# Stick-breaking attention with two heads interleaved, the weight product on GpSimd and 64-column value products

## The reference, cut to what matters

```python
z = jnp.einsum("bhqd,bhkd->bhqk", q_blk, k_pre) * scale
log_rest = jnp.where(strict, jax.nn.log_sigmoid(-z), 0.0)
suffix = lax.cumsum(log_rest, axis=3, reverse=True) - log_rest
a = jnp.where(strict, jnp.exp(jax.nn.log_sigmoid(z) + suffix), 0.0)
outs.append(jnp.einsum("bhqk,bhkd->bhqd", a, v_pre))
```

## Time and profile before

| | |
|---|---|
| median of 3 runs | 2082.38 us |
| time of the profiled execution | 2080.96 us |
| its span, first to last instruction | 2079.2 us |
| busy in the span | PE 2001.2, DVE 1369.4, ACT 884.9, POOL 499.6 us |
| mean granted TensorE clock | 0.99 |
| attention stage, first scan to end of last scan | 871.7 to 1027.5 us |
| first matmul of the output projection | 1034.35 us |

### The profile page before, as it was taken

One profiled execution on the slowest core, in us unless ns is written; L12 is line 12 of the kernel. 1 busy time (PEld: TensorE's weight loads), 2 busy tenths in 40 slices (PEclk: granted clock), 3 DMA queues, 4 the chain that ended last, 5 costly groups with the idle time before them and its releaser, 6 DMA issues. The chain is left out here.

```text
span 2079.2 us, 25150 instructions
## 1 busy us (share of the span) xinstructions
PE 2001.2 (96%) x9345; PEld 1665.9 (80%) x9345; DVE 1369.4 (66%) x1861; ACT 884.9 (43%) x1571; POOL 499.6 (24%) x360
## 2 busy tenths in 40 slices
PE   6999999999999899898899999999999999999997
PEld 5788888887887688787778888887788888878886
DVE  6765565569798532589745565557755655669896
ACT  6433434434445211477634344443434333334443
POOL 1354555430002121000021100121544554510000
PEclk8999999999999999899999999999999999999999
DMA  4223222254400231343234422231232222265102
GB/s 142 81 71 92 81 76 87 86 195 160 146 21 1 86 102 61 102 91 77 54 94 131 132 82 61 62 111 31 84 89 87 82 78 84 77 238 178 61 1 81
DMA packets 216465, 190.14 MB, mean 91 GB/s; under 512 B 7532, under 2 KB 171928, under 8 KB 216344
## 3 DMA queue, kind: packets, MB, share of 16 engines
q1 hardware_dynamic: 216256, 188.51, 29.4%
q10 hardware_dynamic: 88, 0.02, 0.0%
HBM read 152.85 MB, written 35.65 MB: 91 GB/s over the span
## 5 line engine op out<-in xcount | busy, mean ns | idle before, releaser
L1783 DVE TENSOR_TENSOR w_lo<-st,w_hi 128x512 fp32r<-128x512 f32 x160 | 173.2, 1083 | 178.6 <-ACT w_hi L1362 178.5
L917 PE MATMUL ps<-T_hi,w_lo 128*128 128x512 f32 x640 | 249.3, 390 | 0.3 <-issue 0.3
L918 PE MATMUL ps<-T_lo,w_hi 128*128 128x512 f32 x640 | 249.1, 389 | 0.0
L919 PE MATMUL ps<-T_hi,w_hi 128*128 128x512 f32 x640 | 249.1, 389 | 0.0
L917 PE MATMUL ps<-tr_hi,sr_lo 128*128 128x512 f32 x616 | 242.0, 393 | 5.0 <-DVE xT L2014 2.7
L918 PE MATMUL ps<-tr_lo,sr_hi 128*128 128x512 f32 x616 | 240.0, 390 | 0.0
L919 PE MATMUL ps<-tr_hi,sr_hi 128*128 128x512 f32 x616 | 239.9, 389 | 0.0
L917 PE MATMUL ps<-B_hi,w_lo 128*128 128x512 f32 x576 | 227.0, 394 | 10.8 <-DVE B_lo L1783 4.5
L919 PE MATMUL ps<-B_hi,w_hi 128*128 128x512 f32 x576 | 225.9, 392 | 0.0
L918 PE MATMUL ps<-B_lo,w_hi 128*128 128x512 f32 x576 | 225.7, 392 | 0.0
L871 POOL TENSOR_TENSOR ssq<-sq 128x512 f32<-128x512 f32 x6 | 9.5, 1585 | 612.1 <-issue 425.6
(11 more groups left out here) (252 smaller groups left out, 4359.6 us busy)
## 6 DMA issues: line engine op xcount, KB each, us to landing
gate_raw<-in_ffn_w_gate SPq DMA_DIRECT2D x44, 512.0 KB, 5.4
up_raw<-in_ffn_w_up SPq DMA_DIRECT2D x44, 512.0 KB, 5.2
h_spill<-up_s SPq DMA_DIRECT2D x66, 256.0 KB, 2.0
piece_A<-in_ffn_w_down SPq DMA_DIRECT2D x32, 512.0 KB, 4.6
piece_B<-h_spill SPq DMA_DIRECT2D x32, 512.0 KB, 6.0
wa_raw<-in_w_in SPq DMA_DIRECT2D x16, 512.0 KB, 3.9
wb_raw<-in_w_out SPq DMA_DIRECT2D x16, 512.0 KB, 3.9
wb_raw<-in_mem_w_kv SPq DMA_DIRECT2D x16, 512.0 KB, 3.8
```

Of the source, the lines that this page charges most:

```text
L917: pe.matmul(to, w_lo, m_hi, start=first, stop=False, skip_group_check=joins)
L918: pe.matmul(to, w_hi, m_lo, start=False, stop=False, skip_group_check=joins)
L919: return pe.matmul(to, w_hi, m_hi, start=False, stop=last, skip_group_check=joins)
L1783: return dve.tensor_tensor(to, value, plain(hi), ALU.subtract)
```

## The change

- **Two heads at a time.** Tiles come in fours: blocks 0, 1 of head 2p, then 0, 1 of head 2p + 1, then 6, 7 of both, 2, 3 of both, 4, 5 of both. So 16 tiles make one pass (n = 1, 2, 1, 2, 7, 8, 7, 8, 3, 4, 3, 4, 5, 6, 5, 6), and there are 4 passes. q and k have four places for heads in place of two, and aT has 24 blocks in place of 12.
- **Values in column halves.** values(w) handles two heads and two blocks at once: 2b + 2 steps of two matmuls, each of 64 columns of v, one into PSUM rows 0 to 63 and one into rows 64 to 127. There are 16 such calls in place of 32, with as many matmuls in all (160). The splits act_hi and act_lo take all 128 rows, 16 times each in place of 32.
- **Scan.** Its second data operand (whose operation is bypass) is one PSUM column, broadcast, in a bank that nothing writes meanwhile (STILL_BANK).
- **Product on GpSimd.** beta times rest moves from DVE to POOL (pool.tensor_tensor).
- **Transposes.** The lag goes from 3 to 4 tiles. There are two banks in turn in place of three. For tiles with i >= 4 the first four blocks are now copied by DVE (by_dve), the rest by ACT as before.
- **beta in five places** in place of four. Values start 9 tiles behind the scores, and their splits come 10 behind (OUT_LAG), one step after the values on PE.
- **Loads.** A pair's q and k are loaded two pairs ahead, and the first weights of the output projection once 48 tiles' scores are done. The first two tiles of the output projection wait for the last two value splits in the middle of their sums.

```diff
@@ -598,17 +600,36 @@
             holds.update((b, m) for b in range(*z_bank[m]))
         assert all(end <= 4 for _, end in z_bank)
+        def long_tiles(m):
+
+            return sum(tile_at(k)[1] >= 4 for k in range(m + 1))
+
+        STILL_BANK = a_bank[A_PROJ + 4]
+        TURN_BANKS = [b for b in (4, 5, 6) if b != STILL_BANK]
+        assert STILL_BANK != 7
+
         def turns(m):
-
             i = tile_at(m)[1]
-            return [(turns_before[m] + n, 4 + (turns_before[m] + n) % 3, 4 * n, min(4 * n + 4, i + 1))
+            return [(turns_before[m] + n, TURN_BANKS[(turns_before[m] + n) % 2], 4 * n, min(4 * n + 4, i + 1))
                     for n in range(i // 4 + 1)]
+        turn_of = [(m, first) for m in range(M) for _, _, first, _ in turns(m)]
+
+        def by_dve(m, first):
+
+            return tile_at(m)[1] >= 4 and first == 0
+
+        def turned(nth):
+
+            m, first = turn_of[nth]
+            return (s_aT_dve, long_tiles(m)) if by_dve(m, first) else (s_aT, m + 1)
+
         def aT_part(buf, m, lo_, hi_):
-
-            first = AT_FIRST[tile_at(m)[1] // 2]
+            h, i = tile_at(m)
+            first = AT_FIRST[i // 2] + h % 2 * (i // 2 * 2 + 2)
             return buf[:, first + lo_:first + hi_, (m % 2) * P:(m % 2 + 1) * P]
-        STICK_LAG, TURN_LAG, VALUE_LAG = 1, 3, 6
+
+        STICK_LAG, TURN_LAG, VALUE_LAG, OUT_LAG = 1, 4, 9, 10
         def next_splits(m, p):
...
@@ -904,6 +926,13 @@
                     else:
                         ins.then_inc(s_wsum, 1)
+
+            for m in range(M):
+                n = (tile_at(m)[1] + 1) * P
+                pool.wait_ge(s_sig, 2 * (m + 1))
+                pool.wait_ge(s_scan, m + 1)
+                pool.tensor_tensor(beta[m % BETAS][:, 0:n - 1], beta[m % BETAS][:, 0:n - 1], rest[:, m % 3, 1:n],
+                                   ALU.mult).then_inc(s_a, 1)
             for q in range(4, 8):
                 for c in range(DC):
...
@@ -1192,67 +1221,71 @@
                 h, i = tile_at(m)
-                if m % TC == 0:
-                    pe.wait_ge(s_stack[h % 2], 96 * (h // 2 + 1))
+                slot, g = h // 2 % 2, h % 2
+                if m % (2 * TC) in (0, 2):
+                    pe.wait_ge(s_stack[slot][g], 96 * (h // 4 + 1))
+                queries = q_stack[slot][:, g, i * P:(i + 1) * P]
                 if z_free_after[m]:
                     pe.wait_ge(s_sig, 2 * z_free_after[m])
                 n = (i + 1) * P
                 for lo in range(0, n, HALF):
                     keys = slice(lo, min(n, lo + HALF))
                     z = ps[:, z_bank[m][0] + lo // HALF, 0:keys.stop - lo]
-                    pe.matmul(z, q_stack[:, h % 2, i * P:(i + 1) * P], k_lo2[:, h % 2, keys],
-                              start=True, stop=False)
+                    pe.matmul(z, queries, k_lo2[slot][:, g, keys], start=True, stop=False)
                     if keys.stop == n:
                         pe.matmul(ps[:, z_bank[m][0] + lo // HALF, i * P - lo:n - lo], ident_r, neg,
                                   start=False, stop=False)
-                    mm = pe.matmul(z, q_stack[:, h % 2, i * P:(i + 1) * P], k_hi2[:, h % 2, keys],
-                                   start=False, stop=True)
+                    mm = pe.matmul(z, queries, k_hi2[slot][:, g, keys], start=False, stop=True)
                 mm.then_inc(s_z, 1)
             def turn(m):
                 pe.wait_ge(s_a, m + 1)
                 for nth, bank, first, end in turns(m):
-                    if nth >= 3:
-                        pe.wait_ge(s_aT, nth - 2)
+                    if nth >= 2:
+                        pe.wait_ge(*turned(nth - 2))
                     for j in range(first, end):
                         mm = pe.transpose(ps[:, bank, (j - first) * P:(j - first + 1) * P],
-                                          beta[:, m % 4, j * P:(j + 1) * P], ident[:])
+                                          beta[m % BETAS][:, j * P:(j + 1) * P], ident[:])
                     mm.then_inc(s_aT_ps, 1)
             def values(w):
-                h, b = pair_at(w)
-                pe.wait_ge(s_aT, turns_before[2 * w + 2])
+                hp, b = group_at(w)
+                pe.wait_ge(s_aT, 4 * w + 4)
+                if b >= 2:
+                    pe.wait_ge(s_aT_dve, long_tiles(4 * w + 3))
                 if w:
                     pe.wait_ge(s_o_free, w)
-                pair = slice((h // 2) * P, (h // 2 + 1) * P)
-                o = ps[:, 7, (w % 2) * 2 * P:(w % 2 + 1) * 2 * P]
-                for j in range(2 * b + 2):
-                    lo = P if j == 2 * b + 1 else 0
-                    block = AT_FIRST[b] + j
-                    mm = pe.matmul(o[:, lo:], v_all[:, j, pair], aT[:, block, lo:], start=j == 0, stop=j == 2 * b + 1)
+                n = 2 * b + 2
+                for j in range(n):
+                    lo = P if j == n - 1 else 0
+                    for g in range(2):
+                        o = ps[64 * g:64 * (g + 1), 7, (w % 2) * 2 * P:(w % 2 + 1) * 2 * P]
+                        mm = pe.matmul(o[:, lo:], v_all[:, j, hp * P + 64 * g:hp * P + 64 * (g + 1)],
+                                       aT[:, AT_FIRST[b] + g * n + j, lo:], start=j == 0, stop=j == n - 1)
                 mm.then_inc(s_o, 1)
             pe.wait_ge(a_free, z_banks_free)
             pe.wait_ge(s_neg, 2)
             pe.wait_ge(s_ident_r, 1)
-            for s in range(M + VALUE_LAG):
+            for s in range(M + OUT_LAG):
                 if s < M:
                     scores(s)
-                if s < TURN_LAG:
+                if s < len(pool_among):
                     for k in pool_among[s]:
                         pool_map(k)
                 if s == TURN_LAG:
                     pe.wait_ge(a_free, len(a_units))
                 if 0 <= s - TURN_LAG < M:
                     turn(s - TURN_LAG)
-                if s >= VALUE_LAG and (s - VALUE_LAG) % 2 == 0:
-                    values((s - VALUE_LAG) // 2)
-
-
-            pe.wait_ge(s_aT, turns_before[M])
-            pe.wait_ge(s_o_free, W - 2)
+                if VALUE_LAG <= s < M + VALUE_LAG and (s - VALUE_LAG) % 4 == 0:
+                    values((s - VALUE_LAG) // 4)
+
+
+            pe.wait_ge(s_aT, M)
+            pe.wait_ge(s_aT_dve, long_tiles(M - 1))
+            pe.wait_ge(s_o_free, W - 4)
             for step in B_STEPS:
                 k = b_first[step]
                 if step[0] == "tile":
...
@@ -1654,10 +1687,10 @@
                     act.activation(rest[:, s % 3, 0:n], z, ACT.Sigmoid, scale=-SB_SCALE).then_inc(s_sig, 1)
                     if s < NG:
                         act.wait_ge(s_pl, 2 * (s + 1))
-                    if s >= 4:
-                        act.wait_ge(s_aT_ps, turns_before[s - 3])
-                    act.activation(beta[:, s % 4, 0:n], z, ACT.Sigmoid, scale=SB_SCALE).then_inc(s_sig, 1)
-                if s < TURN_LAG:
+                    if s >= BETAS:
+                        act.wait_ge(s_aT_ps, turns_before[s - BETAS + 1])
+                    act.activation(beta[s % BETAS][:, 0:n], z, ACT.Sigmoid, scale=SB_SCALE).then_inc(s_sig, 1)
+                if s < len(pool_among):
                     for k in pool_among[s]:
                         empty(("unit", k))
                 m = s - TURN_LAG
...
@@ -1666,19 +1699,19 @@
                         act.wait_ge(s_spill[slot], 32 * (2 * SBW // P))
                 if 0 <= m < M:
                     for nth, bank, first, end in turns(m):
+                        if by_dve(m, first):
+                            continue
                         act.wait_ge(s_aT_ps, nth + 1)
-                        if m % 2 == 0 and first == 0 and m >= 4:
-                            act.wait_ge(s_o, m // 2 - 1)
+                        if m >= 8:
+                            act.wait_ge(s_o, m // 4 - 1)
                         copy(aT_part(aT, m, first, end),
-                             ps[:, bank, 0:(end - first) * P].rearrange("p (j t) -> p j t", t=P)
-                             ).then_inc(s_aT, 1)
-                if s >= VALUE_LAG and (s - VALUE_LAG) % 2 == 0:
-                    w = (s - VALUE_LAG) // 2
-                    h, b = pair_at(w)
-                    rows = slice(64 * (h % 2), 64 * (h % 2 + 1))
+                             ps[:, bank, 0:(end - first) * P].rearrange("p (j t) -> p j t", t=P)).then_inc(s_aT, 1)
+                if s >= OUT_LAG and (s - OUT_LAG) % 4 == 0:
+                    w = (s - OUT_LAG) // 4
+                    hp, b = group_at(w)
                     act.wait_ge(s_o, w + 1)
-                    copy(a_hi_t[b // 2][rows, h // 2, b % 2 * 2 * P:(b % 2 + 1) * 2 * P],
-                         ps[rows, 7, (w % 2) * 2 * P:(w % 2 + 1) * 2 * P]).then_inc(s_o_hi, 1)
+                    copy(a_hi_t[b // 2][:, hp, b % 2 * 2 * P:(b % 2 + 1) * 2 * P],
+                         ps[:, 7, (w % 2) * 2 * P:(w % 2 + 1) * 2 * P]).then_inc(s_o_hi, 1)
```

(52 more changed lines are left out.)

31 lines of the change are left out of this document (16 added, 15 removed).

## The result

The changed kernel takes **2085.69 us** (median of 20 runs, 2081.78 to 2087.70) against 2081.61 us (20 runs, 2078.72 to 2085.80) for the kernel before: ratio 1.0017, 95% interval 1.0011 to 1.0023. By the forecast's bound of 0.3% that is no change, on the slow side. The forecast was 2066.4, so it was wrong by 19.3 us. The profiled execution has a span of 2084.9, 5.7 above the one before, where the prediction had 16.0 less: 21.7 us to find.

The account below looks back on a forecast made before the run. DVE was taken to bound the stage: 28.8 us of work, 5.7 of waits, gaps and switches made 35.1 a pass against 39.1. Four passes save 16.0: 2080.96 to 2065.0, plus 1.4 gives 2066.4 us; range 2042 to 2094.

Parts of the forecast that it names:

- rival D: POOL's product or its latency binds, or scans pay for POOL beside them: the 4.0 eaten, 2082 us; chance 0.06.
- the term for the switches: PE switching between full and half width may lose matmul overlap: 0 to 1.9 us a pass, taken as 0.6.
- Rival A: Value halves on PE run one after the other: pass 42.3 us, 2097 in all; chance 0.20.
- "5.7" for the waits: DVE runs dry at three places of a pass, walked through the engines' queues: 5.7 us a pass.
- 1, values of b = 3: In the 5, 6, 5, 6 group DVE waits behind PE's values and ACT's act_hi: 2.7 us a pass.
- 2, values of b = 2, and the scan before it: In the 7, 8, 7, 8 group, 6.0 us on PE and ACT against two scans of 4.3: DVE waits 1.7.
- 3, n = 1, 2 beside long turns: With two banks, short tiles wait for DVE's copy and PE's turn: 0.3, and 1.0 behind b = 1's values.
- gaps, switches, late starts: Added to each pass: 0.5 us of gaps, 0.6 for the switches and 0.3 for late starts.
- rival B: PE's waits drop its clock to half, once a pass: 2.5 us each, 10 later, 2076 us; chance 0.14.
- "The end has one more step, but DVE's product is gone from it: 0, plus or minus 2": At the stage's end the added step and the removed DVE product cancel: 0 us, plus or minus 2.
- C: Queues shift until DVE never runs dry: 29.0 us a pass, 40 us less, 2042 in all; chance 0.12.
- the chance of 0.12 for "no change": Chance that the whole kernel measures within about 0.3% (6.2 us) of before, between 2076.2 and 2088.6 us.

Follow-up runs that it names:

- g6: e4 with every value matmul at the full 128 columns of v, both heads added into the same rows: 2086.69 us.
- e4: e1 with the values 11 and their splits 12 tiles behind, in place of 9 and 10: 2066.79 us.
- i1: e4 with ACT's act_hi a step earlier and DVE's split of the output projection's weights a step later: 2057.89 us.
- g5: e4 with the scan's second operand in SBUF again in place of PSUM: 2093.18 us.
- g7: e4 with the product of beta and rest back on DVE, POOL idle: 2107.12 us.
- e2: e1 with PE's waits for transpose banks filled by three unread float32 matmuls at four points of a pass: 2068.25 us.
- e1: The changed kernel with the output projection's first two weights split in step M + 3 in place of M + 2: 2081.27 us.

## Why the prediction was wrong

**The work was right.** DVE: 28.8 forecast less 0.8 for overlap, 27.1 measured (copy 0.68, split 0.42, scans unchanged). POOL: 23.3 forecast, 19.2 measured, inside the bounds of 17.0 to 24.8, and hidden. One of rival D's signs is there, ACT's rest waiting for POOL's product (0.81 at 943.61 and 1.00 at 963.78 in the second pass), but DVE's scans of these two tiles (945.89 and 966.41) start without a wait. ACT: 25 forecast, 25.5. Halves side by side: right (g6 puts their worth at 5.5 us a pass on e4). A call of halves is 0.15 us longer than one in full width, 3.39 against 3.24, and it begins 0.06 to 0.09 later behind the transposes ahead of it (six transposes take 0.77 to the call in i1 and 0.71 in the kernel before, eight take 0.99 in e4 and 0.90 in g6). Four calls a pass make some 0.9, where the term for the switches was 0.6. The Trainium skill (TensorEngine Tiling (Array Packing), Key Properties) says that a change of the tiling mode drains TensorE; if it did, the drain is within these 0.2 us a call. Rival A is refuted by the row at 974.34. D is refuted by the scans' mean of 1340 ns and by g5 and g7, which are slower.

**The step that failed first is "5.7" for the waits**, in two ways. Per pass:

| place | forecast | e2 (clock 1.00) | changed kernel, second pass |
|---|---|---|---|
| 1, values of b = 3 | 2.7 | 4.13 | 4.13 |
| 2, values of b = 2, and the scan before it | 1.7 | 2.07 + 0.81 | 2.07 + 0.81 |
| 3, n = 1, 2 beside long turns | 1.3 | 1.96 | 3.66 |
| n = 3, 4 beside long turns | 0 | 0.95 | 2.72 |
| sum | 5.7 | 9.9 | 13.4 |
| DVE's work | 28.0 | 27.0 | 27.1 |
| gaps, switches, late starts | 1.4 | 0 | 0 |
| pass | 35.1 | 36.96 | 40.4 |

- *Mis-sized, 4.2 a pass.* The walk of place 1 had PE's values begin 1.0 us after DVE's scan of n = 4; they begin 1.93 after it (972.41 to 974.34), since PE first waits for a bank and has a whole tile's scores and transposes still to do. The split came 8.4 after that start and not 7.2. At places 2 and 3 the forecast was 1.2 and 0.7 short; which step of the walk these come from was not taken apart. And the fourth place is the same as the third: whoever finds a wait behind long tiles in one group has to look at the other group that stands behind long tiles.
- *The clock, 3.4 a pass.* This is rival B, given 0.14 and 2.5 us a pass for one drop. The rows were at hand: the waits of 2.01 and 1.47 that stood before a drop, and a walk that said PE would wait up to 2.5 us. The changed kernel has two pairs of waits of 1.4 to 2.0 a pass, and one or two drops. e2 shows the price: 1.7 for a drop (3.0 for the long one of the first pass, whose copies wait 4.92 where e2's wait 1.96), where B had 2.5. Whether three transpose banks in place of two would take the waits away was not tried.

Against these 7.6 stand 2.3 that DVE's work, the gaps and the late starts were forecast too high, so a pass is 5.3 above its forecast. Yet first to last scan is only 13.0 above (3.0 saved where 16.0 were forecast), not 4 x 5.3: three whole passes lost 1.3 each against before, and what is outside them took 31.6 us in place of 38.5. Nearly all of that is the first pass: from the first scan to that of the 17th tile it takes 32.5 (871.73 to 904.22), before 40.0 (871.66 to 911.63). The prediction multiplied a steady pass by four and had no term for the start.

**"The end has one more step, but DVE's product is gone from it: 0, plus or minus 2"** failed by the most in one place: the tail is 8.9 longer. e1 takes 5.4 of them back (15.7 to 10.3; 4.4 in the medians): the weights' step, M + 2, which the prediction never held against the new TURN_LAG. It counted the end's own steps and not what is queued between them. The other 3.5 probably come with the longer lags; that is not shown, since no part of them was tried alone in the changed kernel.

Together: 13.0 in the passes and 8.9 in the tail are 21.9, against the 21.7 to be found. The range (2042 to 2094) held the result, but by luck: it was stretched for A and C, and D's own range (2077 to 2090), which holds it too, had a cause that did not come. None of the rivals had the waits, the clock and the tail at once; each was priced alone, and so the chance of 0.12 for "no change" had no room for three misses in a row. The forecast's own range, 2056 to 2077, was also narrower than its terms: added up on the late side (5, 2, 2 and 7) they reach 2082.

**DVE as the bound: right in e4, not in the changed kernel.** In the changed kernel waits make a third of DVE's pass, so DVE's work does not set it. In e4 it does: 12 us more work on DVE lengthen the pass by 10.0 to 11.4 (g7, at a lower clock). A pass of 35.1 was to be had, since e4 has 34.70, but that the two agree so well is luck: e4 has 26.8 of work and 7.8 of waits, the forecast had 28.0, 5.7 and 1.4 for gaps and switches. The forecast erred in taking the lags as they are for harmless.

## What to carry to other kernels

Where a lag of a software pipeline is changed, look at every step that is pinned to a number of its own (here M + 2) and at both groups that stand behind the long tiles: the order in the queues was worth 27.8 us here (2085.69 to 2057.89), with the same work on every engine. Once TensorE's own work no longer fills a stage, its waits can bring its clock down, so price a pair of long waits on PE (1.36 to 1.60 us here) with what runs behind it at half clock. Taking such a wait away can be worth more than its own length: in e1 a wait 2.4 us shorter made the tail 5.4 shorter, in i1 3.2 made 4.2. Filling the waits was worth 3.4 us a pass (e2). Before believing in a gain from moved work, walk the tail too.
